# Every fourth slot's value rows summed by VectorE instead of TensorE in a two-layer PEER diffusion backbone

## What is computed

```python
def peer(h, wq, subkeys, u_tab, v_tab):
    q = (t @ wq).reshape(-1, PEER_HEADS, 2, PEER_QDIM // 2)
    s = jnp.einsum('thpd,hpkd->thpk', q, subkeys)
    sv, si = lax.top_k(s, PEER_TOPK)
    cand = sv[:, :, 0, :, None] + sv[:, :, 1, None, :]
    cv, ci = lax.top_k(cand.reshape(..., PEER_TOPK * PEER_TOPK), PEER_TOPK)
    ...
    idx = i1 * PEER_KEYS + i2
    g = jax.nn.softmax(cv, axis=-1)
    def block(args):                       # 128 tokens
        tb, ib, gb = args
        act = jax.nn.gelu(jnp.einsum('td,thkd->thk', tb, u_tab[ib]))
        return jnp.einsum('thk,thkd->td', gb * act, v_tab[ib])
```

## Time and profile before

| | us |
|---|---|
| runs of the kernel before (3) | 2379.73, 2381.09, 2384.25 |
| median | 2381.09 |
| the profiled execution | 2382.0 |
| its span, first to last instruction | 2380.2 |
| TensorE, VectorE, ScalarE, GpSimd busy | 2080.4 (87%), 1629.1 (68%), 961.4 (40%), 1021.0 (43%) |
| bytes moved | 940.46 MB, mean 395 GB/s; the gathers 805.36 MB of it |

### The profile page before, as it was taken

One profiled execution on the slowest core, in us unless ns is written; L12 is line 12 of the kernel. 1 busy time (PEld: TensorE's weight loads), 2 busy tenths in 40 slices (PEclk: granted clock), 3 DMA queues, 4 the chain that ended last, 5 costly groups with the idle time before them and its releaser, 6 DMA issues.

```text
span 2380.2 us, 23945 instructions
## 1 busy us (share of the span) xinstructions
PE 2080.4 (87%) x6792; PEld 1119.3 (47%) x6792; DVE 1629.1 (68%) x3980; ACT 961.4 (40%) x2788; POOL 1021.0 (43%) x868
## 2 busy tenths in 40 slices
PE   8988998899998988988899998898799987777777
PEld 6775554455564434544454454335456532222222
DVE  2876768967766568788856668754665887766444
ACT  2113434543334444444454334534443444443333
POOL 0002444444334544444445445520233555566774
PEclk9998999999999999999999999999899999999999
DMA  9968999999999999999999999994599999999997
GB/s 402 420 252 320 394 415 421 414 422 422 421 421 421 412 421 405 421 419 420 389 406 422 421 421 421 421 381 192 224 403 379 415 421 421 422 421 421 421 421 319
DMA packets 132738, 940.46 MB, mean 395 GB/s; under 512 B 14736, under 2 KB 17936, under 8 KB 18960
## 3 DMA queue, kind: packets, MB, share of 16 engines
q0 software_dynamic: 110592, 805.36, 82.0%
q1 hardware_dynamic: 22032, 133.73, 13.7%
HBM read 937.98 MB, written 1.05 MB: 395 GB/s over the span
## 4 chain that ended last, share of the span: by engine, by line
PE 36%; DMA 29%; DVE 16%; issue 7%; POOL 6%; ACT 4%; SPq 0%; POOLq 0%; DVEq 0%; ACTq 0%
DMA uv<-uv_dram,stage_idx 28%; PE psum L948 18%; PE psum L762 9%; POOL uv L1019 6%; DVE uv L1557 6%; PE psum L744 4%; DVE h L1250 2%; PE psum L893 1%; DMA h<-c_rows_dram 1%; ACT diag L1193 1%; ACT wv L1191 1%; PE psum L680 1%; ACT gel L1189 1%; DVE work L1521 0%; PE psum L922 0%
## 5 line engine op out<-in xcount | busy, mean ns | idle before, releaser
L948 PE MATMUL psum<-uv,diag 128*128 128x512 f32 x3072 | 1449.8, 612 | 240.0 <-ACT diag L1193 221.8
L1019 POOL DMA_INDIRECT uv<-uv_dram,stage_idx x768 | 987.2, 1285 | 1051.7 <-PE psum L948 823.7
L1557 DVE CUSTOM_DVE_ANT_0 uv<-uv,h 128x1024 f32<-128x1024 f32 x768 | 935.2, 1226 | 538.1 <-DMA uv<-uv_dram,stage_idx 527.4
L948 PEld LDWEIGHTS psum<-uv,diag 128*128 128x128 f32 x3072 | 562.7, 193 | 1023.7 <-issue 518.1
L1189 ACT ACTIVATE gel<-dots 128x1 f32<-128x1 f32 x768 | 156.3, 203 | 1052.4 <-DVE dots L1557 1050.2
L1193 ACT ACTIVATE diag<-const,wv 128x128 f32<-128x128 f32 x768 | 309.8, 403 | 24.8
L762 PE MATMUL psum<-hT,wring 128*128 128x256 f32 (+1 forms) x1280 | 266.2, 362 | 1.5 <-ACT hT L1060 1.5
L762 PEld LDWEIGHTS psum<-hT,wring 128*128 128x128 f32 x1280 | 227.9, 191 | 59.7 <-issue 33.0
L1191 ACT ACTIVATE wv<-gel,gw 128x1 f32<-128x1 f32 x768 | 228.0, 297 | 25.1
L1005 POOL COPY stage_idx<-idx 128x8 uint32 (+1 forms) x96 | 33.6, 350 | 284.6 <-DVE idx L1529 283.9
L1042 ACT ACTIVATE work<-psum 128x256 f32<-128x256 f32 (+2 forms) x122 | 47.8, 393 | 137.6 <-PE psum L762 108.5
(11 more groups left out here) (216 smaller groups left out, 1289.2 us busy)
## 6 DMA issues: line engine op xcount, KB each, us to landing
uv<-ada_dram SPq DMA_DIRECT2D x25, 1024.0 KB, 17.1
wring<-in_dram SPq DMA_DIRECT2D x24, 1024.0 KB
wring<-wq_dram SPq DMA_DIRECT2D x24, 1024.0 KB
uv<-uv_dram,stage_idx POOLq DMA_INDIRECT x768
uv<-ada_t_dram SPq DMA_DIRECT2D x11, 1024.0 KB, 16.7
uv<-in_dram SPq DMA_DIRECT2D x10, 1024.0 KB, 18.9
wring<-ada_dram SPq DMA_DIRECT2D x7, 1024.0 KB
wring<-ada_t_dram SPq DMA_DIRECT2D x5, 1024.0 KB
```

The lines of the kernel that those rows point to most:

```text
L948: last = mm(acc[:, b, :], diag[:, s % RING, :], uv[:, s % RING, D + 512 * b:D + 512 * (b + 1)], start=(c == 0), stop=(c == NSEL - 1))
L1019: nc.gpsimd.indirect_dma_start(out=uv[:, s, :], out_offset=None, in_=tables[stage // 2], in_offset=bass.IndirectOffsetOnAxis(ap=stage_idx[ ...
L1557: v.tensor_tensor_reduce(out=uv[:, r, 0:D], in0=uv[:, r, 0:D], in1=h2[:, row_of[stage], t, :], scale=1.0, scalar=0.0, op0=ALU.mult, op1=AL ...
```

## The change

In 128 of the 768 slots, every fourth (c % 4 == 3) in a range of each tile, the value rows no longer go through `diag` and TensorE. VectorE multiplies them with the weights `wv` and adds them to `own_sum[T]`, a buffer of 128 x 1024 floats which is at that time free in each tile (scratch, halves of `h2`, rows of the context stream). In such a slot (a taken slot, below) TensorE makes one product of 4 columns with zeros (`silu_c` columns of 0), which adds nothing to `acc` and counts up `uv_used` once VectorE's addition has counted up `rows_added`; ScalarE makes no diagonal. Some slots after the last of a tile the step `own_sum` (`join_own_sum`) multiplies the sum with the gate and adds it to `x`. Slots taken: 24, 4, 26, 22, 24 and 28 in tiles 0 to 5.

```diff
--- before.py
+++ after.py
@@ -61,6 +61,20 @@
 QW = P // QUAD
 
 
+
+
+OWN_SUMS = {0: (4, 100, 108), 1: (60, 78, 80), 2: (4, 108, 114), 3: (20, 108, 114), 4: (4, 100, 108), 5: (4, 116, 120)}
+
+
+def by_vector(s):
+    T, c = s // NSEL, s % NSEL
+    return T in OWN_SUMS and OWN_SUMS[T][0] <= c < OWN_SUMS[T][1] and c % 4 == 3
+
+
+def by_tensor(s):
+
+    return sum(not by_vector(i) for i in range(s + 1))
+
 PARTS = [("ident", P), ("c", KC * 2), ("b_ada", 2 * 48), ("norm_g", 2 * 2 * KC), ("gather_sums", 4),
          ("iota", TOPK), ("cos", TT * 32), ("sin", TT * 32), ("a_conv", MC * CONV_A), ("c_conv", MC * CONV_C), ("c_conv_b", MC),
          ("c_norm_g", MC), ("vnorm_g", MIX), ("qk_g", 2 * HD), ("subln_g", P), ("lam", 4 * HD),
@@ -193,7 +207,7 @@
 DVE_TAKES = ("ac_cols", "ab_cols", "spatial", "ca_cols", "out_rows", "out_half", "out_heads")
 TAKE_AFTER = 2
 
-NEED_NONE = ("gate_diag", "mods", "lam", "v_scale", "conv", "qk_scale", "rope", "rms_root", "ada_row", *ACT_TAKES, *DVE_TAKES)
+NEED_NONE = ("own_sum", "gate_diag", "mods", "lam", "v_scale", "conv", "qk_scale", "rope", "rms_root", "ada_row", *ACT_TAKES, *DVE_TAKES)
 
 
 def needs(step, left):
@@ -267,6 +281,7 @@
     placed += spread(rms(1, (0,)) + [("norm_ctx", 2, 0)] + deal(convolve_2, heads_2) + gate(2, 0)
                      + [("out_half", 2, 0, b, t) for b in range(2) for t in range(TT)], at + 131, at + 246)
     placed += spread(gate(2, 1), 2 * STAGE_SLOTS + 40, 2 * STAGE_SLOTS + 60)
+    placed += [(T * NSEL + slot, ("own_sum", T)) for T, (_, _, slot) in OWN_SUMS.items()]
     placed.sort(key=lambda p: p[0])
 
     program, todo = [], list(placed)
@@ -492,6 +507,9 @@
         late_search = Search(h2_1, 512, (h2_1, 0), (1,))
         row_of = (0, 1, 1)
 
+        own_sum = {0: view(work, 7680, D), 1: h2[:, 1, 1, :], 2: h2[:, 0, 1, :], 3: x[:, 0, :], 4: x[:, 1, :],
+                   5: x[:, 0, :]}
+
         c_rows = h2[:, 0, :, :]
         row_tmp = h2[:, 1, :, :]
 
@@ -548,7 +566,7 @@
         dots_ready, gelu_ready, wv_ready, diag_ready, uv_used = (
             sem(s) for s in ("dots_ready", "gelu_ready", "wv_ready", "diag_ready", "uv_used"))
 
-        acc_free = sem("acc_free")
+        acc_free, rows_added = sem("acc_free"), sem("rows_added")
         x_rows_ready, out_stored = sem("x_rows_ready"), sem("out_stored")
 
         program = schedule()
@@ -943,7 +961,12 @@
                 T, c = s // NSEL, s % NSEL
                 if c == 0 and T:
                     pe.wait_ge(acc_free, T)
-                pe.wait_ge(diag_ready, s + 1)
+                if by_vector(s):
+
+                    pe.wait_ge(rows_added, n.up("rows_added"))
+                    mm(acc[:, 0, 0:4], ident, silu_c[:, 0, 4:8], start=False, stop=False).then_inc(uv_used, 1)
+                    return
+                pe.wait_ge(diag_ready, by_tensor(s))
                 for b in range(2):
                     last = mm(acc[:, b, :], diag[:, s % RING, :], uv[:, s % RING, D + 512 * b:D + 512 * (b + 1)],
                               start=(c == 0), stop=(c == NSEL - 1))
@@ -1557,6 +1582,31 @@
                 v.tensor_tensor_reduce(out=uv[:, r, 0:D], in0=uv[:, r, 0:D], in1=h2[:, row_of[stage], t, :], scale=1.0, scalar=0.0,
                                        op0=ALU.mult, op1=ALU.add, accum_out=dots[:, r:r + 1]).then_inc(dots_ready, 1)
 
+            def add_rows(s):
+
+                if not by_vector(s):
+                    return
+                T, r = s // NSEL, s % RING
+                dve.wait_ge(wv_ready, s + 1)
+                rows = uv[:, r, D:2 * D]
+                if n.up(("rows", T)) == 1:
+                    done = v.tensor_scalar(own_sum[T], rows, wv[:, r:r + 1], None, ALU.mult)
+                else:
+                    dve.wait_ge(rows_added, n["rows_added"])
+                    done = v.scalar_tensor_tensor(out=own_sum[T], in0=rows, scalar=wv[:, r:r + 1], in1=own_sum[T], op0=ALU.mult, op1=ALU.add)
+                done.then_inc(rows_added, 1)
+                n.up("rows_added")
+
+            def join_own_sum(T):
+                stage, t = T // TT, T % TT
+                dve.wait_ge(rows_added, n["rows_added"])
+                dve.wait_ge(*taken["gate", stage, 1])
+                link(v.tensor_tensor(own_sum[T], own_sum[T], gate_peer[:, :], ALU.mult))
+                row = x[:, tile_of(stage, t), :]
+                link(v.tensor_tensor(row, row, own_sum[T], ALU.add))
+
+            steps["own_sum"] = join_own_sum
+
             def close(T):
 
                 stage, t = T // TT, T % TT
@@ -1576,7 +1626,7 @@
             v.memset(ones[:, :], 1.0)
             v.memset(silu_c[:, :, :], 0.0).then_inc(constants_set, 1)
             dve.wait_ge(const_loaded, 16)
-            walk(steps, dot, nothing, close, takes)
+            walk(steps, dot, add_rows, close, takes)
 
 
 def in_columns(w):
```

## The result

The changed kernel takes 2431.42 us (median of 4 runs, 2429.66 to 2435.47), the kernel before 2381.32 beside it (2379.73 to 2384.25). The ratio is 1.0211, 95% interval 1.0194 to 1.0229: 50 us slower. The prediction said 2387.6, with a range from 2374 to 2397. The sign was right and the size was not: 6 us were forecast and 50 came.

A forecast was written before the change was run, and what follows sets the result against it. DMA at 422 GB/s was taken as the bound, except in openings, a gap and dents. Terms 3.5 + 0.5 + 2.5 = 6.5 us, added to the profiled run and corrected to the median, gave 2387.6 us, range 2374 to 2397.

The forecast's parts named there:

- the cover: Steady stretches: gathers issued some 15 us before landing, 5.7 needed; the 9 us spare makes freeing 3.5 us later cost nothing.
- The openings: First 50 slots of stages 2 and 0: TensorE and VectorE take turns, leaving 3.5 us and 0.5 us of loss.
- give back 1.3 us: Taken slots within TensorE's backlog: each saves 1.3 us of TensorE work and reduces its lateness by that.
- slot 519: Stage 2 opening: first slot followed, with TensorE done 1.4 us later because the addition stands behind a dot.
- The dents: Stretches at 440 to 480, 920 to 960, 1120 to 1200 us: VectorE just full with the additions, +2.5 us.
- VectorE becomes the bound: Rival, chance 0.15: ring already empty in the dents, carried work passed on, 9 us there; 2394 us.
- The addition 1.25 us: VectorE at each taken slot: one 128x1024 operation of 1.25 us, between 1.22 and 1.30.
- the small product 0.45 us: TensorE at each taken slot: one 128x4 product in two passes, 0.45 us, replacing 1.75 us.
- The joins: End of each tile's taken slots: two VectorE operations of 1.23 us, hidden where VectorE waits for landings.
- The relief arrives: Rival, chance 0.24: in both openings TensorE's lighter load brings back half the lost DMA time; 2373 us.
- The rule on GpSimd's issues: Gather issues beside VectorE additions: held up by up to 1 us, nothing in the sum, at worst 2 to 3 us.
- What would show it: Signs: TensorE waiting at small products, rate below 389 over 1709 to 1865 us, profile from slot 560 moved 3 to 6 us.

The follow-up runs named there:

- adds_only: Kernel before, TensorE multiplying all slots, with VectorE's 128 additions and joinings made on token rows and never reaching x: 2394.2 us.
- own_free: Changed kernel with a semaphore for every fourth ring place, raised by VectorE behind its addition; GpSimd waits for it, TensorE passes over taken slots: 2387.6 us.
- tile5_only: Changed kernel with only the 28 additions of tile 5, none in the other tiles: 2381.1 us.
- no_openings: Changed kernel with tiles 0 and 4 taken only from their slot 48 on: 2415.3 us.
- open_after: Changed kernel with additions only in slots 4 to 47 of tiles 0 and 4, 22 of them: 2399.8 us.
- late_free: Kernel before, no additions; at the 128 taken slots the places s, s+1 and s+2 are freed together behind the products of s+2: 2413.4 us.
- own_early: own_free with the addition of slot s moved right behind the dot of s+1: 2385.5 us.
- open_own_3: own_early with additions only in tile 0 to slot 75, tile 4 to slot 63, and tile 3: 2379.42 us, ratio 0.9986.
- tile1_only: Changed kernel with only tile 1's four slots and its joining taken: 2387.3 us.
- relief_only: Changed kernel without the taken slots' additions and joins, TensorE waiting only for ScalarE's weight; their values are missing from the result: 2378.8 us.

## Why the prediction was wrong, point by point

The measured parts: additions +13 (adds_only), relief in their company -7 (own_free less adds_only), the wait in TensorE's order +44 (changed kernel less own_free), together 50. They add up by construction, and each rests on single executions, good to some 4 us. Alone the relief can't be told from nothing.

- **"A gather is issued some 15 us before its landing, against the 5.7 needed, so I cost it at nothing: the cover is 9 us."** This step failed, and it is most of the miss. The 15 us and the 9 us were right for the quiet tile and so was the 0 there (tile5_only). It failed twice over. Only the taken place was costed, 3.5 us late (measured 3.8), not the two behind it in TensorE's order (4.9 and 5.2 at slot 715). And the cover was taken from the quiet tile, while the trace of the kernel before already had places in tiles 0 to 4 with only 1.3 to 4.1 us of it. It ran out in tile 1, which was put at nothing, and in tile 2. Measured outside the openings: +34 (no_openings), additions and relief included, where 2.5 was forecast.
- **The openings, 3.5 + 0.5.** That the wait costs there was right, the size was not: 18.5 (open_after). With additions and relief but no wait it is 0 (own_free, by the dots), so the term that was mis-sized is what stays of TensorE's lateness. Why it is so large is shown in part. late_free, with the clock at 1.00 over its second opening, is 5 us late by slot 48 and 7 more from slot 512 to 592, so late freeing can cost some 12 us there at the full clock. The sum also let each taken slot in the backlog give back 1.3 us and had no term for the clock, which was 0.92 over the slots of the second opening against 1.00 before; what that costs there no run separates. Within the sum slot 519 comes out 2.0 us late by its own rows, not 1.4, which is too little to matter.
- **The dents, +2.5, and the rival that VectorE becomes the bound, 9.** The load alone is 13 over the whole kernel, but 7 of it arise in the openings; the 6 elsewhere lie between the sum and the rival and decide for neither. VectorE is nearly as full as worked out (76.6 of 80 us from 400 to 480 us in own_early, where the sum had 79.8). The prediction let TensorE's shorter backlog pay some of it back; it pays 7 over the whole run.
- **The addition 1.25 us, the small product 0.45 us.** 1.28 us, and 2 x 0.28 = 0.56. Right within 0.1 us.
- **The joins, at nothing.** No run isolates them. In tile5_only one cost nothing.
- **The relief arrives, 0.24.** It does not in this form: TensorE's busy time fell in both openings and the rate with it. Without the wait, and with additions in tiles 0, 3 and 4 alone (open_own_3), 2.7 us of the forecast 8 arrive.
- **The rule on GpSimd's issues.** The prediction took its row for the work of one two-input operation beside it, but the dots themselves do the same: in the kernel before, 59 issues met no instruction of VectorE and took 0.94 us, and most of those in the quiet tile, which begin 0.1 us into a dot, took 1.92. In between an issue grows with what is left of the dot when it begins (1.12 us with 0.2 to 0.4 us left, 1.71 with 0.8 to 1.0). The Trainium skill, SBUF — State Buffer, "SBUF: two separate sides", has the two exclude each other; this trace agrees, and the dots did it before the additions came. The additions brought no more of it: the mean issue took 1190 ns against 1285 before, with 128 more long operations on VectorE, with fewer issues beside a dot (438, before 519). No run here shows a cost of it in the time.
- **"What would show it".** TensorE waiting at the small products and the rate below 389 at 1709 to 1865 us came as written, though part of the fall to 323 is the shift of the slots; 367 is the rate of the same slots. The profile from slot 560 on is the old one moved, but by 50 us, not 3 to 6. The share lost in tiles 1 and 2 had no place in that list.

What stays open: how the 44 us of the wait divide between the freeing as such and the waits that VectorE gets back from TensorE. late_free shows 32 without any addition to wait for, but delays the places in another pattern. How much the lower clock adds is open too.

## What to carry to other kernels

When one in-order engine waits for another on behalf of one item, cost every item queued behind the wait, and compare the sum with what is left of a shared reserve after the worst neighbouring burst, not with what the quietest stretch shows. A semaphore for the resource itself, waited on by the engine that refills it, costs a few lines and here removed 44 of 50 us. Work taken off an engine that isn't the bound was worth nothing here, and even where it was the bound, 25 us of it bought 3.

## What the runs showed of the hardware

In the quiet tile of the changed kernel TensorE stops at every fourth slot, for 2.9 us on average and 5.3 at the longest, and the granted clock is at the lower of its two levels (1.2 GHz) for part of the time: 0.85 on average in the window at 2200 us against 1.00 before. In tile1_only the slot behind a wait of 3.93 us took 3.76 us, against 1.98 for one at full clock. The Trainium skill, TensorE: Matmul & The Clock Gate, "What's actually happening", says that a gate halves the clock when the engine has lately been idle; the trace agrees. In relief_only, where it doesn't wait for VectorE and only has less to do, the mean granted clock is 0.936 against 0.975, and 0.87 in that same window:

```profile
2200.00:2240.00 40.00, 28.60 (x56) 11.45 (x56) 19.98 (x33) 12.78 (x44) 24.02 (x19) 0.87 1.02 422
```

TensorE is busy 28.6 us there and was 31.7, though 16 of the 64 wide passes are gone and 8 of the small ones came: part of what was taken off came back as slower work.
